# A hybrid mixer and expert layer on one core: split modulation, token-major attention outputs, compact states, decays among the projections

## The reference

```
u = x * (1 + scale1) + shift1
[x_lru | gate | q | k | v | g | a_low] = u @ w_in          # 512 512 256 256 512 512 16
x_lru = conv over 4 columns of each grid row
h = sum over 2 directions of scan(a * h + b),  a, b from sigmoids of x_lru @ block weights
y_lru = h * gelu(gate)
# gated linear attention, 4 heads, dk 64, dv 128, chunks of 64 tokens in column-major grid order
la = log_sigmoid(a_low @ gla_wa[d] + gla_ba[d]) / 16;  bcum = cumsum(la) in a chunk
scores = mask(q exp(bcum) @ (k exp(-bcum)).T);  o = scores @ v + q exp(bcum) @ S
S = exp(btot) * S + (k exp(btot - bcum)).T @ v             # from chunk to chunk, both directions
y_gla = o * rsqrt(mean(o^2) + eps) * gla_norm_g * silu(g)
x = layer_norm(alpha * x + gate1 * ([y_lru, y_gla] @ w_out))
h = x * (1 + scale2) + shift2
x = layer_norm(alpha * x + gate2 * sum of top 4 of 32 SwiGLU experts of h)
```

## Time and profile before

| | |
|---|---|
| median of 3 runs | 3049.19 us (3049.18 to 3050.3) |
| the profiled execution | 3068.91 us, span 3067.2 us, granted TensorE clock 0.909 of full |
| TensorE matmul / VectorE / ScalarE / POOL busy | 2675.6 / 831.1 / 539.8 / 243.5 us |
| DMA | 567.35 MB, mean 185 GB/s |

### The profile page before, as it was taken

How to read it: one execution, slowest core, us unless ns; L and a number is a source line. 1 busy time by engine, 2 the same in 40 slices (tenths; PEclk the granted TensorE clock), 3 DMA queues, 4 the chain that set the end, 5 groups by cost and what they waited for, 6 DMA issues and landing times.

```text
span 3067.2 us, 29137 instructions
## 1 busy us (share of the span) xinstructions
PE 2675.6 (87%) x8073; PEld 1292.6 (42%) x8074; DVE 831.1 (27%) x1176; ACT 539.8 (18%) x573; POOL 243.5 (8%) x274
## 2 busy tenths in 40 slices
PE   8999999484767718999999899999999999999992
PEld 8433444272634413444434343444444444444441
DVE  1102431548323311122221222122222222222225
ACT  1003442313101101112111211111111111111110
POOL 0000110000011240000000100000000000000100
PEclk9999999665578758999999999999999999999996
DMA  7600000000031134658694798992699845686653
GB/s 288 206 0 8 21 28 21 0 1 0 0 125 62 49 147 162 233 209 313 233 372 153 272 407 304 407 331 87 226 346 348 311 171 193 230 337 231 242 192 131
DMA packets 177566, 567.35 MB, mean 185 GB/s; under 512 B 17797, under 2 KB 34553, under 8 KB 177402
## 3 DMA queue, kind: packets, MB, share of 16 engines
q1 hardware_dynamic: 162362, 524.29, 44.9%
q0 software_dynamic: 15168, 42.57, 5.5%
HBM read 537.36 MB, written 33.64 MB: 186 GB/s over the span
## 4 chain that ended last, share of the span: by engine, by line
PE 80%; DVE 7%; issue 6%; DMA 4%; ACT 2%; POOL 1%; POOLq 1%; SPq 0%; DVEq 0%; ACTq 0%
PE psall L507 28%; PE psall L536 14%; PE psall L634 10%; PE psall L522 5%; PE psall L550 4%; PE psall L728 4%; DMA arena<-h_rows,lruw 3%; PE psall L558 3%; PE psall L628 2%; PE psall L595 2%; PE psall L574 2%; PE psall L704 1%; DVE arena L1121 1%; PE psall L618 1%; DVE arena L1136 1%
## 5 line engine op out<-in xcount | busy, mean ns | idle before, releaser
L507 PE MATMUL psall<-arena 128*128 128x512 f32 x1984 | 875.1, 602 | 31.8 <-issue 31.8
L507 PEld LDWEIGHTS psall<-arena 128*128 128x128 f32 x1984 | 380.9, 193 | 505.7 <-issue 505.7
L536 PE MATMUL psall<-arena 128*128 128x512 f32 x992 | 437.2, 599 | 0.0
L1299 DVE TENSOR_TENSOR arena<-psall,arena 64x512 f32<-64x512 f32 (+1 forms) x67 | 62.7, 936 | 1083.5 <-PE psall L507 839.9
L634 PE MATMUL psall<-arena 128*128 128x512 f32 (+3 forms) x656 | 315.3, 642 | 0.0
L536 PEld LDWEIGHTS psall<-arena 128*128 128x128 f32 x992 | 188.4, 192 | 227.3 <-issue 227.3
L522 PE MATMUL psall<-arena 128*64 128x512 f32 x1152 | 261.1, 612 | 25.4 <-issue 21.6
L928 ACT COPY arena<-psall 128x1024 f32<-128x1024 f32 x48 | 48.6, 1013 | 1046.2 <-PE psall L558 1046.2
L634 PEld LDWEIGHTS psall<-arena 128*128 128x128 f32 (+1 forms) x656 | 122.3, 187 | 184.1 <-issue 179.4
L558 PE MATMUL psall<-ident,arena 128*128 128x128 f32 x712 | 98.0, 280 | 90.2 <-DMA arena<-h_rows,lruw 84.8
L522 PEld LDWEIGHTS psall<-arena 128*64 128x64 f32 x1152 | 96.4, 141 | 178.4 <-issue 178.4
(11 more groups left out here) (246 smaller groups left out, 2046.1 us busy)
## 6 DMA issues: line engine op xcount, KB each, us to landing
arena<-in_w_gate_dram SPq DMA_DIRECT2D x128, 1024.0 KB
arena<-in_w_up_dram SPq DMA_DIRECT2D x128, 1024.0 KB
arena<-in_w_down_dram SPq DMA_DIRECT2D x128, 1024.0 KB
arena<-in_w_ada_dram SPq DMA_DIRECT2D x12, 2048.0 KB, 8.1
arena<-in_b_gate_dram SPq DMA_DIRECT2D x32, 512.0 KB
arena<-in_b_up_dram SPq DMA_DIRECT2D x32, 512.0 KB
arena<-in_b_down_dram SPq DMA_DIRECT2D x32, 512.0 KB
arena<-in_w_in_dram SPq DMA_DIRECT2D x16, 512.0 KB, 3.9
```

Source lines behind the costliest of these rows:

```text
L507: mm = pe.matmul(ps[2 * g + s], xT[:, k, :], ring[q][:, k % 2, s * BANK:(s + 1) * BANK], start=(k == 0), stop=(k == KD - 1))
L536: mm = pe.matmul(ps[6 + s], aT[:, k, :], ring[GUP + k // 2][:, k % 2, s * BANK:(s + 1) * BANK], start=(k == 0), stop=(k == KD - 1))
L1299: mm = dve.tensor_tensor(gb[p0:p1, 0:n], psG[p0:p1, 0:n], ebias[p0:p1, 0, c0:c0 + n], ALU.add)
```

## The change

- **Split modulation.** shift1 and scale1: all four pieces are loaded at once, and streamed against the two columns of `csil`, two pieces side by side in two column groups; the rows are copied out and turned by sixteen small transposes. The other four vectors: sixteen steps (`ada` in the plan) among the LRU steps, each with two 512 KB blocks of `w_ada` (`wada2`, one buffer pair) streamed against one column of `csil`, into a free part of bank 7; the two rows are stored to DRAM and loaded again, broadcast, after the last.
- **Projections.** The convolution tiles come first and read `uT` contiguously; the evictions write the row-major order, VectorE's taps of both latent halves after the second. `v` follows, then k, a_low, q, gate, g. Each LRU step has four jobs and two `ada` steps. The ring of weight tiles has three places instead of five. Taps, scans and products stay.
- **Decays among the projections.** The first pair's logits, logarithms, scans and exponentials are put among the gate and g jobs (`prep`); the second pair's run beside the first pair's states and outputs. Query and key factors have a buffer each.
- **Compact states.** Both heads of a pair lie on 128 partitions (`gS` without the head index); TensorE computes only the needed quarters, in groups of chunks with one semaphore step per group, and VectorE makes one update per chunk and direction.
- **Token-major outputs.** Scores are stationary and V streams, so tokens are on the partitions; ScalarE's Square accumulates the sum per token, the root and reciprocal are of 128x16, the scaling goes with a copy, and the result is turned back by TensorE and multiplied once by weight and gate.
- **w_out** has a place of its own and is loaded as soon as the keys of the second pair are turned.
- **Job table.** An expert's half job, where there is one, comes first, not last.

The core of the diff:

```diff
-            for j in range(4):
-                pe.wait_ge(d_wada[j % 3], 16 * (j // 3 + 1))
-                for m in range(4):
-                    q = 4 * j + m
-                    for k in range(KD):
-                        mm = pe.matmul(ps[1][:, 2 * q:2 * q + 2], wada_ring[:, j % 3, k, m * P:(m + 1) * P],
-                                       csil[:, k, :], start=(k == 0), stop=(k == KD - 1))
+            for jp in range(2):
+                for b in range(2):
+                    pe.wait_ge(d_wada[2 * jp + b], 16)
+                for k in range(KD):
+                    for b in range(2):
+                        mm = pe.matmul(ps[1 + jp][64 * b:64 * b + 2, :], csil[:, k, :], wada1[2 * jp + b][:, k, :],
+                                       start=(k == 0), stop=(k == KD - 1), skip_group_check=True)
                 mm.then_inc(ada_used, 1)
...
-            for j in range(4, 12):
...
-                for k in range(KD):
-                    mm = pe.matmul(ps[2 + j % 2][:, :], csb[:, k, :], wada_ring[:, j % 3, k, :],
-                                   start=(k == 0), stop=(k == KD - 1))
...
-        plan, at_job = [("job", i) for i in range(NT + NTC + 3)], NT + NTC + 3
+        plan, at_job, at_ada, NADA = [("job", i) for i in range(3)], 3, 0, 16
         for lstep in range(2 * JL):
-            plan += [("gate_r", lstep), ("job", at_job), ("gate_i", lstep), ("decay", lstep), ("job", at_job + 1),
-                     ("job", at_job + 2), ("scan", lstep)]
-            at_job += 3
-        plan += [("job", i) for i in range(at_job, len(jobs))]
+            plan += [("gate_r", lstep), ("job", at_job), ("ada", at_ada), ("job", at_job + 1), ("gate_i", lstep),
+                     ("decay", lstep), ("job", at_job + 2), ("ada", at_ada + 1), ("job", at_job + 3), ("scan", lstep)]
+            at_job += 4
+            at_ada += 2
+        prep = [("z", 0), ("z", 1), ("zln", 0), ("zln", 1), ("cum", 0), ("cum", 1), ("eqk", 0), ("gqk", 0), ("eqk", 1),
+                ("gqk", 1)]
+        for i in range(at_job, len(jobs)):
+            plan.append(("job", i))
+            if prep:
+                plan.append(prep.pop(0))
...
+                if what == "ada":
+                    pe.wait_ge(d_adaw, 32 * i + 32)
+                    pe.wait_ge(lru_sig, 3 * i + 3)
+                    for k in range(KD):
+                        for b in range(2):
+                            mm = pe.matmul(ps[7][64 * b:64 * b + 1, CTX:CTX + P], csil[:, k, 0:1],
+                                           wada2[b][:, k, :], start=(k == 0), stop=(k == KD - 1), skip_group_check=True)
+                    mm.then_inc(ada2_mm, 1)
...
-                                       moving(kind, k, seg), start=(k == 0), stop=(k == KD - 1))
+                                       uT[:, k, seg[0]:seg[1]], start=(k == 0), stop=(k == KD - 1))
...
+                for n in STATE_GROUPS[g]:
+                    T, c = order[d][n] // 2, order[d][n] % 2
+                    for h in range(2):
+                        mm = pe.matmul(ps[2 * d + c][64 * h:64 * h + 64, (n // 2 % 4) * DV:(n // 2 % 4 + 1) * DV],
+                                       gKT[64 * c:64 * c + 64, d, T, 64 * h:64 * h + 64],
+                                       V[64 * c:64 * c + 64, T, (2 * pr + h) * DV:(2 * pr + h + 1) * DV],
+                                       start=True, stop=True, skip_group_check=True)
...
+                        pe.matmul(o_at(T, h), gSc[:, T % 2, h, d, :],
+                                  V[:, T, (2 * pr + h) * DV:(2 * pr + h + 1) * DV], start=(d == 0), stop=False,
+                                  skip_group_check=True)
...
+                    for c, h in ((0, 0), (1, 1), (0, 1), (1, 0)):
+                        ch = 2 * T + c
+                        mm = pe.matmul(o_at(T, h)[64 * c:64 * c + 64], gQ[pr][64 * h:64 * h + 64, d, ch * CH:(ch + 1) * CH],
+                                       gS[64 * h:64 * h + 64, d, slot(order[d].index(ch)), :], start=False,
+                                       stop=(d == 1), skip_group_check=True)
...
+            sp.wait_ge(ke_turned, 10)
+            sp.dma_start(wout, w_out[0].rearrange("(k p) n -> p k n", p=P)).then_inc(d_wout, 16)
+            sp.wait_ge(gla_done, 32)
             sp.wait_ge(gla_done, 4)
-            sp.dma_start(wout, w_out[0].rearrange("(k p) n -> p k n", p=P)).then_inc(d_wout, 16)
...
-            link(dve.tensor_tensor(U[:, 9:10], U[:, 6:7], U[:, 4:5], ALU.is_lt))
+            link(dve.tensor_tensor(U[:, 9:10], U[:, 6:7], U[:, 4:5], ALU.is_ge))
```

More of the change, by code:

```diff
@@ L291, in layer @@
         CA = CG + HEADS * DV
-        jobs = [("v", T, None, None) for T in range(NT + NTC)]
+        jobs = []
         tiles = [("conv", j, j * P, P) for j in range(JL)]
@@ L707, in _ @@
-                    mm.then_inc(o_mm, 1)
-                for h in range(2):
-                    pe.wait_ge(sq_ready, 2 * pr + h + 1)
-                    for s in range(2):
-                        pe.matmul(ps[6 + s][:, :], ones[:, :], gSq[:, h, s * BANK:(s + 1) * BANK],
-                                  start=True, stop=True).then_inc(rms_mm, 1)
-                    if h == 0:
-                        pe.wait_ge(rms_act, 4 * pr + 2)
+                        scores(pr, T + 1)
+                    outputs(pr, T)
@@ new lines, in scaled @@
+            def scaled(pr, T, h):
+                return act.activation(gN[:, T, h, :], o_at(T, h),
+                                      ACT.Copy, scale=rr[:, 2 * T + h:2 * T + h + 1])
+            keys_out(0)
+            for d in range(2):
+                logit_size(1, d)
+            for d in range(2):
+                log_term(1, d)
+            for d in range(2):
+                decays(1, d)
+            for T in range(NT):
+                squares(0, T)
+            keys_out(1)
+            root(0)
@@ L895, in std @@
+            act.wait_ge(rr_ready, 1)
+            for T in range(NT):
+                for h in range(2):
+                    mm = scaled(0, T, h)
+                mm.then_inc(on_act, 1)
+            for T in range(NT):
+                squares(1, T)
+            root(1)
+            act.wait_ge(rr_ready, 2)
+            for T in range(NT):
+                scaled(1, T, 0).then_inc(on_act, 1)
             def std(n):
@@ L1032, in _ @@
                     yh = grid_half(YT[:, j], seg)
[L1033 removed]
+                    dve.tensor_tensor(yh, yh, half(gelu_[:, (2 * j + seg[0] // BANK) % 2]), ALU.mult).then_inc(gated, 1)
                 if by_act[i]:
@@ new lines, in causal @@
+            def causal(pr, T):
+                dve.wait_ge(sc_mm, NT * pr + T + 1)
+                if T >= 2 or pr:
+                    dve.wait_ge(o_mm, NT * pr + T - 1)
+                if T < 2 and not pr:
+                    dve.wait_ge(gla_const, 2)
+                for h in range(2):
+                    dve.copy_predicated(gSc[:, T % 2, h], masks[:, :, :],
+                                        ps[2 * (T % 2) + h][:, 0:2 * P].rearrange("p (d b) -> p d b", d=2)).then_inc(sc_ready, 1)
@@ new lines, in _ @@
+            logit_min(1, 0)
+            for d in range(2):
+                states(0, 0, d)
+            logit_min(1, 1)
+            for g in range(1, 3):
+                for d in range(2):
+                    states(0, g, d)
+            for T in range(NT):
+                causal(0, T)
+                if T in (1, 3):
+                    cumulate(1, T // 2)
+                if T in (5, 7):
+                    decayed(1, T // 2 - 2)
+            invert(0)
+            for g in range(3):
+                for d in range(2):
+                    states(1, g, d)
```

674 lines of the change are left out of this document (393 added, 281 removed).

## The result

The changed kernel took 2770.8 us (median of 4 runs, 2768.3 to 2772.76), beside 3049.7 of the kernel before on the same chip: 0.9074 of its time, interval 0.9045 to 0.9103. Forecast were 2852, with a range of 2806 to 2898. Its profiled execution has a span of 2767.4 us at a granted clock of 0.938.

The account below looks back on a forecast made before the run. TensorE time was taken to bound up to 556 us, latency from 556 to 847, then one load. Start -77, projections +3.5, attention -107, w_out load -12, experts -5 summed to -197.5: 2869.7 profiled, 2852 median, range 2806 to 2898.

Parts of the forecast that it names:

- the attention term: Gated-linear-attention stage: 183 us forecast against 290.6 before, so -107; bounds 133 and 225.
- I take half clock: Attention stage: TensorE assumed at half clock; at full clock the sum would be some 45 us lower.
- the price of the small records: Attention tiles: sixteen quadrant records priced at 2.3 us of a 5.2 us tile, at half clock.
- TensorE's 152 records at 145 ns are 22: Attention state updates: TensorE's records take 22 us per pair, above 14.5 for VectorE; 29 with last group and logits.
- Experts: Expert stage: half job leading its expert frees the weight ring during a full job; -5 us, bounds -20 and +15.
- The shift from profile to median: Whole kernel: median 19.7 us below the profiled span, applied to the forecast: 2869.7 becomes 2852.
- Projections: Projection stage: 423.5 us against 420.5, contiguous convolution reads' -55 offset by taps, row modulation, logits and LRU chain.
- later tiles lie under 14 us of matmuls: Projections: strided evictions and taps cost only the first convolution tile, +4 us; later ones are covered.
- Rival B: Projections: in-order queues cost 5 us every step, row modulation nearer L574's record; +35 to +90, about 2905; chance 0.20.
- Rival C: TensorE: changing array shapes empties the array, some 56 more at 0.15 to 0.35 us; +8 to +20, 2866; chance 0.10.
- Rival D: Row modulation: 512 one-column records go singly with exposed weight loads, making the kernel slower than before; chance 0.02.
- Rival A: Attention: dense enough for full clock, quadrants overlap; another 30 to 50 us off, 2810; chance 0.17.

## Why the prediction was wrong, and where it was right

**The clock, and with it the attention term (-107, measured -179.5).** The step that failed is "I take half clock"; a second one is the price of the small records. The first read the 50 us at 0.50 of the earlier trace rows as what "streams like these" get. But the new loop isn't the old one: the eight records per head that streamed 64 columns against the states (L704) have become quadrant records of 128 columns, and it ran at 1.00 in both pairs from its second tile on, but for 3 us behind the wait at 522.28. Which of its parts brings the clock isn't shown; cutting its products with V into pieces takes it away. Its phases, forecast against measured: logits 9, 9.6; states 29 and 25, 17.3 and 14.7; tiles 46 and 42, 26.3 and 19.0; keys 8, 4.8; output turns and gating 10, 8.4; tail 14, 11.0. The tiles missed by 43 us. Measured at half clock a tile takes about 4.2 us (2.00 + 1.07 + 1.15), not 5.2, so 16 of it was the price; the other 27 are the clock (2.33 instead of 4.2 us, less what waits took back). The price stood on sixteen quadrant records at 145 ns each, and they came at 1.07 / 16 = 67 ns. The Trainium skill, "TensorE: Matmul & The Clock Gate", Part 1, says that the throttled clock is the default and sustained activity releases it. The prediction wrote that the trace disagreed; by the time this rule gave, some 45 us lower, it would have come nearer, and the new loop, once it ran without a wait, agrees with it. What the runs don't bear out is that being busy by the profile is enough: the cut kernels were busy without a pause at 0.50.

**States.** "TensorE's 152 records at 145 ns are 22" was mis-sized in the same way. The chunk products go out in quadrants, first at a granted clock of 1.00, then at 0.50:

```profile
488.34 1.98 PE L727 MATMUL psall<-arena 64*64 64x128 f32 x64 [0.77 <-ACT arena L987]
...
495.57 1.99 PE L727 MATMUL psall<-arena 64*64 64x128 f32 x32 [1.85 <-DVE arena L1279]
```

That is 31 ns each at full clock and 62 at half, so 152 of them are under 9.5 us at either, and VectorE's updates pace the phase: 36 per pair and two copies, 0.36 us and a gap of 0.02 each in the chain, close to the 14.5 us that the prediction had worked out for VectorE and then passed over for the larger number.

**Experts (-5, measured -31.6).** By the runs that change the order alone, it is worth 25.6 us (before) and 22.4 (changed); the other 6 to 9 us are about what two traces of the kernel before differ by there, 6.7. The direction was right, and that the ring frees under a full job was named, but not that late gathers are what it spares. The prediction took no price from the waits for gathered rows, though TensorE had 22.5 us of them in nine places, and settled on -5 with no row behind it. The bound of -20 would have been the better value.

**The shift from profile to median (-19.7).** The prediction carried the offset of the median over to the changed kernel. It belonged to the kernel before, for the most part to its tile loops, which sometimes change their clock, and the change rewrites them: the changed kernel's profile and median differ by 1.2 us. That the offset was kept made the miss look 20 us smaller, which is luck. The prediction also held that 6 us is what a measurement can tell; single runs of the kernel before spread over 56.

**Projections (+3.5, of which the stage's own sum is +3; measured +1.2): right in sum, by compensation.** A modulation step took 1.84 us, not 2.6 (58 ns a record, near the lower bound of 55), 12 us less in sixteen. The taps cost more: "later tiles lie under 14 us of matmuls" overlooked context jobs of 3.6 us and LRU work in the same queue; three waits of 15.1 us together, and some 5 more of half clock and missing busy time, stand against 12 forecast for taps and LRU chain together. Rival B was right that queues served in order can make TensorE wait, and wrong that they do so at every step: TensorE was busy 406.7 of 421.7 us, with one wait for ScalarE in sixteen steps.

**Right.** The start (57.0 against 59, the longest term but one) and `w_out` (-10.3 against -12; 8.8 by its own run). Rival C, an array emptied at each change of shape for 0.15 to 0.35 us, has no room: a job of 512 columns takes 6.97 us behind a modulation step (111.54 to 118.51) and 6.95 behind LRU gates, which don't change the shape (120.66 to 127.61). Rival D fell with the 58 ns. Rival A, full clock and overlapping quadrants at 2810, had the mechanism; with the experts' 27 us it would have been within 15 of the measurement, though in part by the 20 us of the offset, since its 30 to 50 us are less than the 72 that attention gave.

## What to carry to other kernels

The granted clock depends on what a loop issues, and a loop can be one that runs at either: if a change rewrites a loop of small matmuls, work out both clocks, and treat the half clock of the old loop as evidence for the old loop alone. Where a kernel's own runs spread over tens of microseconds, look first for a loop whose clock differs between two profiles, and carry no offset from it across a change. In a kernel that gathers rows while weights stream, put the short job where the ring is full, and price the wait by the rows that show a late gather.

## What the runs showed that was not expected

- A loop with TensorE busy 99.9% of the time by the profile can stay at 1.2 GHz for 45 us (granted 0.50), and twelve more records per tile brought another one to 2.4 GHz: more work in 4.81 us than the less in 6.46.
- The same program, the same loop, changes clock at 671 us in one execution, at 798 in another; the runs spread by 56 us.
- A record with one column of weights and 128 streamed columns, in two column groups, takes 58 ns; chunk products in four quadrants take 31 ns at full clock and 62 at half.
- The profile gives 221 ns to each read of ScalarE's accumulator, next to 288 for the square of 128x128, but the two overlap: a square and its read go out every 0.25 us (from 579.06 to 579.31, for one), so eight take about 2 us in the chain:

```profile
L997 ACT ACTIVATE arena<-psall 128x128 f32<-128x128 f32 x32 | 8.3, 288 | 37.4 <-PE psall L755 37.4
...
L997 ACT ACTIVATION_READ_ACCUMULATOR arena<-psall 128x1 f32 x32 | 7.1, 221 | 0.0
```
